# Sample attention over paged caches: a page on 64 partitions instead of 32

## The reference

```python
def mla_attend(q_lat, q_pe, q_pos, ckv, kpe, k_pos):
    s = (jnp.einsum("bqhc,bkc->bhqk", q_lat, ckv, preferred_element_type=jnp.float32)
         + jnp.einsum("bqhr,bkr->bhqk", q_pe, kpe, preferred_element_type=jnp.float32)) * MLA_SCALE
    s = jnp.where(k_pos[None, None, None, :] <= q_pos[None, None, :, None], s, -jnp.inf)
    p = jax.nn.softmax(s, axis=-1).astype(ckv.dtype)
    return jnp.einsum("bhqk,bkc->bqhc", p, ckv)
...
        ckv_past = cache_ckv[l, page_table].reshape(DB, past, KV_LORA)
        kpe_past = cache_kpe[l, page_table].reshape(DB, past, QK_ROPE)
```

## Time and profile before

| | us |
|---|---|
| time, median of 3 runs | 2335.02 (2325.26 to 2335.15) |
| profiled execution, its own time | 2333.65 |
| its span, first to last instruction | 2331.9 |
| PE busy | 2203.8 (95% of the span) |
| weight loads | 2010.6 (86%) |
| DVE, ACT, POOL busy | 1181.7, 831.7, 282.1 |

### The profile page before, as it was taken

One profiled execution on the slowest core, in us unless ns is written; L12 is line 12 of the kernel. 1 busy time (PEld: TensorE's weight loads), 2 busy tenths in 40 slices (PEclk: granted clock), 3 DMA queues, 4 the chain that ended last, 5 costly groups with the idle time before them and its releaser, 6 DMA issues.

```text
span 2331.9 us, 52276 instructions
## 1 busy us (share of the span) xinstructions
PE 2203.8 (95%) x22086; PEld 2010.6 (86%) x22086; DVE 1181.7 (51%) x1942; ACT 831.7 (36%) x1530; POOL 282.1 (12%) x275
## 2 busy tenths in 40 slices
PE   8989999999999999999999899999999989999997
PEld 7966667799998999999988666677999989999997
DVE  4732223533458763566667322244333687626665
ACT  4322223423235431234443222244232454313334
POOL 0012220000016000000340122200000340000002
PEclk9979999999999999999999799999999999999999
DMA  6167882022253222224432687800222522322252
GB/s 239 62 195 284 289 284 99 13 81 81 81 163 97 91 89 91 67 84 150 140 122 74 230 292 290 291 32 21 88 81 84 175 82 91 102 72 75 86 175 79
DMA packets 69362, 304.46 MB, mean 131 GB/s; under 512 B 8465, under 2 KB 13457, under 8 KB 56785
## 3 DMA queue, kind: packets, MB, share of 16 engines
q1 hardware_dynamic: 45360, 164.79, 22.0%
q0 software_dynamic: 18432, 125.84, 15.1%
q10 hardware_dynamic: 5408, 11.47, 1.5%
HBM read 294.02 MB, written 4.90 MB: 128 GB/s over the span
## 4 chain that ended last, share of the span: by engine, by line
PE 84%; DVE 7%; DMA 3%; ACT 2%; issue 2%; ACTq 0%; DVEq 0%; SPq 0%
PE PS L950 59%; PE PS L1206 7%; PE PS L1221 5%; DVE m_WL L1424 2%; PE PS L1190 2%; PE PS L1357 1%; DMA m_QSR<-m_QSF 1%; DMA m_WS<-in_w_units 1%; PE PS L1160 1%; PE PS L1184 1%; PE PS L1335 1%; PE PS L1346 1%; DVE m_X L1458 1%; DVE m_XL L1469 1%; ACT m_WH L511 1%
## 5 line engine op out<-in xcount | busy, mean ns | idle before, releaser
L950 PE MATMUL PS<-m_XH,m_WH 128*128 128x288 f32 x2560 | 733.5, 299 | 35.2 <-DVE m_WL L1424 19.4
L950 PE MATMUL PS<-m_XL,m_WH 128*128 128x288 f32 x2560 | 726.3, 296 | 0.0
L950 PE MATMUL PS<-m_XH,m_WL 128*128 128x288 f32 x2560 | 581.9, 297 | 0.0
L950 PEld LDWEIGHTS PS<-m_XH,m_WH 128*128 128x128 f32 x2560 | 485.1, 189 | 41.8 <-DVE m_WL L1424 22.8
L950 PEld LDWEIGHTS PS<-m_XL,m_WH 128*128 128x128 f32 x2560 | 485.8, 190 | 0.8
L1424 DVE TENSOR_TENSOR m_WL<-m_WS,m_WH 128x1024 fp32r<-128x1024 f32 (+2 forms) x284 | 369.0, 1301 | 230.3 <-ACT m_WH L511 220.4
L950 PEld LDWEIGHTS PS<-m_XH,m_WL 128*128 128x128 f32 x2560 | 424.6, 189 | 0.0
L511 ACT ACTIVATE m_WH<-m_WS 128x1024 fp32r<-128x1024 f32 (+2 forms) x284 | 315.1, 1112 | 299.2 <-PE PS L950 282.0
L950 PE MATMUL PS<-m_HH,m_WH 128*128 128x288 f32 x704 | 205.7, 299 | 7.7 <-DVE m_WL L1424 7.2
L950 PE MATMUL PS<-m_HL,m_WH 128*128 128x288 f32 x704 | 203.4, 296 | 0.0
L1206 PE MATMUL PS<-m_RAWF,m_QSR 32*64 32x128 f32 x4608 | 159.6, 285 | 27.9 <-issue 25.9
(11 more groups left out here) (287 smaller groups left out, 3315.2 us busy)
## 6 DMA issues: line engine op xcount, KB each, us to landing
m_WS<-in_w_units SPq DMA_DIRECT2D x232, 512.0 KB
m_WS<-in_w_units SPq DMA_DIRECT2D x48, 704.0 KB
m_WS<-in_w_units SPq DMA_DIRECT2D x4, 576.0 KB
out_y<-m_X SPq DMA_DIRECT2D x8, 288.0 KB, 2.2
m_QSR<-m_QSF ACTq DMA_DIRECT2D x4, 384.0 KB
m_RAWF<-in_cache_wide,m_IDXS POOLq DMA_INDIRECT x96
m_BRI<-in_branch_in ACTq DMA_DIRECT2D x2, 760.0 KB, 6.4
m_CST<-in_consts SPq DMA_DIRECT2D x1, 1425.5 KB, 12.6
```

Of the source, the lines that this page charges most:

```text
L950: mm = pe.matmul(out(half), w(part, k), x(k)[:, half_of(half)], start=(k == 0 and part == 0 and x is xh), stop=(k == last and part == 1))
```

## The change

A page now lies on 64 partitions. A gathered row holds the latent of two positions (512 numbers), 64 rotary numbers and, in the wide cache, 512 numbers by feature: a gather of 128 rows brings 2 pages, so a unit has **four gathers** of half the size, 576 or 1088 numbers a row, and `g_landed` counts four.

The by-feature keys stand in 4 groups of 64 features; the partitions 64h to 64h+63 hold page `h` of a gather. Scores of a group are 8 products of 128 columns on **four tiles of 64x64**, with `QSF` where the block matches and with one rotated copy `QSR` where it doesn't (two DMAs instead of six). The rotary part is on tiles of 32x64 still, 16 products of 64 columns a unit, in two parts `j` (the even and the odd positions); the second waits on a semaphore for the first's end (`even_mm`), now in units by feature too. A unit by feature has 32 + 16 products instead of 72. A unit by row has 16 rotary products instead of 8; its transposes, latent products and values are as many as before.

All scores now take two banks of 256 columns, in turn (`score_bank`): 0 and 1 for a unit by row, 2 and 3, then 0 and 1, then 4 and 5. So in every unit by feature two groups and half the rotary part stand ahead of the wait for `s_exp`, and in a unit by row half the key transposes do. DVE and ACT read two banks of 256 columns in every unit. On the host the caches are laid out anew, and the index list has 64 partitions to a page.

The core of the diff:

```diff
-GP = 4
+GP = 2
 NG = PAGES // GP
-NU2 = DB * NG // 2
+NQ = 4
+NU2 = DB * NG // NQ
 NF = 3
-ROW = 4 * KL + P
+HP = P // 2
+ROW = 2 * KL + HP
 KEYS_AT = ROW
-FROW = ROW + 8 * P
+FROW = ROW + 4 * P
...
-        RAWT = at("RAWT", [P, 2, ROW], F32, r_z + 6 * TB)
-        RAWF = [at(f"RAWF{n}", [P, 2, FROW], F32, o) for n, o in enumerate((r_xs, r_xs + 2 * FROW * 4, r_w))]
-        assert 4 * FROW * 4 <= 2 * DT * TB
-        QSR = [at(f"QSR{c}", [P, KT, 512], F32, r_w + 2 * FROW * 4 + (c - 1) * 4096) for c in range(1, 4)]
-        assert 2 * FROW * 4 + 3 * 4096 <= 6 * UW * 4
+        RAWT = at("RAWT", [P, NQ, ROW], F32, r_z + 6 * TB)
+        RAWF = [at(f"RAWF{n}", [P, NQ, FROW], F32, o) for n, o in enumerate((r_xs, r_xs + NQ * FROW * 4, r_w))]
+        assert 2 * NQ * FROW * 4 <= 2 * DT * TB
+        QSR = at("QSR", [P, KT, 512], F32, r_w + NQ * FROW * 4)
+        assert NQ * FROW * 4 + 4096 <= 6 * UW * 4
...
+        def score_bank(u):
+
+            return (0, 2, 0, 4)[u % 4]
+
+        def score_banks(u):
+
+            return PS[:, score_bank(u):score_bank(u) + 2, 0:256]
...
-                    for half in range(2):
-                        g = b * NG + half * 4 + j
+                    for q in range(NQ):
+                        g = b * NG + NQ * j + q
                         pool.indirect_dma_start(
-                            raw_of(u)[:, half, :], None, source.rearrange("l n c -> (l n) c"),
+                            raw_of(u)[:, q, :], None, source.rearrange("l n c -> (l n) c"),
                             bass.IndirectOffsetOnAxis(ap=IDXS[:, l, g:g + 1], axis=0))\
                             .then_inc(S[f"g_landed{u % 4}"], 16)
...
-                for c in range(1, 4):
-                    for to, at0, n in ((0, 32 * c, P - 32 * c), (P - 32 * c, 0, 32 * c)):
-                        act.dma_start(QSR[c - 1][to:to + n, :, :], QSF[at0:at0 + n, :, :]).then_inc(S["qs_turned"], 16)
+                for e in range(2):
+                    act.dma_start(QSR[64 * e:64 * e + 64, :, :], QSF[64 - 64 * e:128 - 64 * e, :, :])\
+                        .then_inc(S["qs_turned"], 16)
...
+                def rope_scores(u, j, start=False, stop=False):
+
+                    if j == 1:
+                        pe.wait_ge(S["even_mm"], l * NU2 + u + 1)
+                    rows_of = slice(u // 4 * 64, (u // 4 + 1) * 64)
+                    for half in range(2):
+                        for c in range(2):
+                            for h in range(2):
+                                rows = slice(64 * h + 32 * j, 64 * h + 32 * j + 32)
+                                at0 = half * P + j * HP
+                                mm = pe.matmul(PS[64 * c:64 * c + 64, score_bank(u) + h, at0:at0 + HP], QSP[rows, rows_of],
+                                               raw_of(u)[rows, 2 * half + c, 2 * KL:ROW],
+                                               start=(start and half == 0), stop=(stop and half == 1))
...
                 def scores_by_feature(u, groups):
 
-                    q = slice(u // 4 * 64, (u // 4 + 1) * 64)
+                    rows_of = slice(u // 4 * 64, (u // 4 + 1) * 64)
                     for g in groups:
-                        for s in range(4):
-                            rows = slice(32 * s, 32 * s + 32)
-                            if g < 8:
-                                ct, c = g // 4, (g - s) % 4
-                                weights = QSF[rows, ct, q] if c == 0 else QSR[c - 1][rows, ct, q]
-                                at0 = KEYS_AT + g * P
-                            else:
-                                weights, at0 = QSP[rows, q], 4 * KL
-                            for half in range(2):
-                                mm = pe.matmul(PS[64 * half:64 * half + 64, 2 + s, 0:P], weights,
-                                               raw_of(u)[rows, half, at0:at0 + P], start=(g == 0), stop=(g == 8))
-                    return mm
+                        for half in range(2):
+                            for c in range(2):
+                                for h in range(2):
+                                    rows = slice(64 * h, 64 * h + 64)
+                                    weights = (QSF if g % 2 == h else QSR)[rows, g // 2, rows_of]
+                                    at0 = KEYS_AT + g * P
+                                    pe.matmul(PS[64 * c:64 * c + 64, score_bank(u) + h, half * P:(half + 1) * P], weights,
+                                              raw_of(u)[rows, 2 * half + c, at0:at0 + P],
+                                              start=(g == 0 and half == 0), stop=False)
...
-                        rope_scores(u, (0, 2))
+                        rope_scores(u, 0, start=True)
+                        turn_keys(u, 0)
                         pe.wait_ge(S["s_exp"], l * NU2 + u)
-                        turn_keys(u, 0)
                         turn_probs(u - 1)
                         turn_keys(u, 1)
-                        rope_scores(u, (1, 3))
+                        rope_scores(u, 1)
                         scores(u)
-                    elif u % 4 == 1:
+                    else:
                         if u == 1:
-                            pe.wait_ge(S["qs_turned"], (l + 1) * 96)
-                        scores_by_feature(u, range(0, 5))
+                            pe.wait_ge(S["qs_turned"], (l + 1) * 32)
+                        scores_by_feature(u, (0,))
+                        rope_scores(u, 0)
+                        scores_by_feature(u, (1,))
                         pe.wait_ge(S["s_exp"], l * NU2 + u)
                         if u == 1:
                             pe.wait_ge(S["in_set"], l + 1)
                         turn_probs(u - 1)
-                        scores_by_feature(u, range(5, 9)).then_inc(S["s_mm"], 1)
-                    else:
-                        pe.wait_ge(S["s_exp"], l * NU2 + u)
-                        turn_probs(u - 1)
-                        scores_by_feature(u, range(0, 9)).then_inc(S["s_mm"], 1)
+                        scores_by_feature(u, (2, 3))
+                        rope_scores(u, 1, stop=True).then_inc(S["s_mm"], 1)
```

81 lines of the change are left out of this document (36 added, 45 removed).

## The result

The kernel after takes 2278.62 us (median of four, 2267.57 to 2280.5) where the kernel before takes 2331.79: a ratio of 0.9766, with a 95% interval of 0.974 to 0.9792. It is faster by 2.3%, where 2386 us was forecast. That is within 6 us of the lower end of rival A. The profiled execution has a span of 2275.9 us, 56.0 less than before's.

The account below looks back on a forecast made before the run. TensorE (PE) was taken as the bound, held back beside POOL's gathers. Per layer +25.8 feature units, +1.8 row units, +1.1 last units, -3.0 start gave +25.7; two layers +51 on 2335.0 made 2386 us, range 2295 to 2440.

Parts of the forecast that it names:

- rival A: Units by feature: slow stretch doesn't grow with the gathers, 2297 us, or disappears, 2273; chance 0.19.
- Supply: Units by feature: 100 records must precede the values, slowed until 6.05 us; 8.1 us a unit instead of 6.87.
- slow stretch: Sample attention: while POOL writes gathers, PE gets 7.4 records a us instead of over 60, after some 45 in reserve.
- rival B: Attention stage: PE's clock drops in the longer thin stretch, units lose 1.6 us, 2420 to 2453 us; chance 0.16.
- Gathers: POOL, each unit: four gathers of about 948 ns replace two, taking 4.7 us instead of 2.2.
- Own work: Units by feature, PE's work with nothing beside it: 5.4 us against 4.85 before, tile shape changes included.
- Unit by row: Eight more rotary products add 0.25 us to 6.8; bounds 0 and 0.8 us.
- Start of the stage: Wait on rotated query copies goes, VectorE's copies come next: about 3 us a layer saved, 0 to 4.
- Landing: Gather queue: four units of 7.9 MB in 31.3 us want 250 GB/s of 357, so no price.
- sign that half the packet size costs bandwidth: PE waiting for a gather's landing would show the forecast wrong; no size given.
- The lower end of the case: Units by feature at 7.4 us, with 100 records out by 5.35 us: +22 us, 2357 in all.
- Work ahead of the exponentials: Units by feature: new score banks let PE work ahead of this wait; worth little, 0.12 us stand there.

Follow-up runs that it names:

- after_again: Kernel after, unchanged, measured again: 2479.49 us, ratio 1.056 to the kernel before.
- before_again: Kernel before, unchanged, profiled again in one execution: 2317.37 us.
- session 3: Kernel after, unchanged (2479.49 us), and with its first rotary part moved behind the turned probabilities (2485.32 us), beside the kernel before at 2346.2 us.
- probs_first: Kernel after with the wait on the exponentials and the turned probabilities ahead of all scores in units by feature: 2492.93 us, ratio 1.0637.
- after_more: Kernel after, unchanged, measured a third time: 2287.66 us, ratio 0.9803 to the kernel before.
- pair_2: Kernel before with its latent score groups paired into products of 256 columns (wrong scores), rerun in another session: 2254.13 us, ratio 0.969.
- split_2: Kernel after with each score product cut into two of 64 columns, rerun in another session: 2332.82 us, ratio 1.0013.
- pair256: Kernel before with its latent score groups paired into products of 256 columns (wrong scores), first run: 2301.74 us, before 2356.78.
- four_half: Kernel before with each gather issued as two gathers of half rows, products unchanged: 2538.12 us, before 2356.78.
- held: Kernel before with each unit's gathers held until two thirds of the running unit's scores are out: 2350.94 us, ratio 1.0083.
- before_still: Kernel before without gathers for units by feature from unit 4 of a layer on (wrong result): 2375.73 us, before 2356.78.
- held_3: Kernel before with gathers held until two thirds of the running unit's scores are out, third run: 2379.24 us, ratio 1.0194.

## Why the prediction was wrong

**What failed** is the step named *Supply*. It took a slow stretch at 7.4 records a us with a reserve of 45 as a property of the two kernels, from one profiled execution, and let it grow with POOL's time to 6.05 us into the unit. The first profile of before ran in the way with the trickle. The measured result of after ran in the way without it, where four gathers hold nothing back and a unit takes 5.47 us (5.69 on average) instead of the 8.1 of the forecast. The weight of rival A (0.19) was set by which rows spoke for the slow stretch, and all rows came from one execution. The Trainium skill (Runtime: NRT & Kernel Launch, Instruction fetch mechanics), which states that the fetching of instructions is hidden, was set aside there because the 82.8 us of the earlier trace rows spoke against it; in the profile of after, 17.2 us at the score line agree with it, in after_again 118.9 do not. The 3.03 us in before_again, which end 1.40 us after a 16 KB packet of instructions, speak for a third case, in which the fetch of a block isn't hidden.

**Where the mechanism applies, it was undersized.** In session 3 the stop comes where forecast (a few dozen records after the first gather), but the unit takes 9.45 us and not 8.1 or 8.4. From the third gather on the pauses grow to 0.99 to 1.11 us, so about 3.4 records a us pass (5 in 0.46 and 0.99 us) and not 7.4, and rival B comes on top: the clock was 0.85 over the stage, and in some units the value products took 3.61 us, at 1.2 GHz, instead of 1.88. The unit by row, put at +0.25, took 8.20. So 2479 lies above even rival B's 2420 to 2453, which had the forecast's unit and the clock together.

**Point by point** otherwise, from the profile of after:

- *Gathers*: 256, of 947 and 957 ns in the median; forecast 948. Right.
- *Own work*: 5.4 us forecast, 5.47 measured; the last two units 5.4 forecast, 5.47 where they don't wait. Right, with the price of a change of tile shape in it. The sum took before's last two units at 4.85 each; the last one took 6.21 and 6.24 there, with the stops at 367 and 1521 us in it.
- *Unit by row*: +0.25 forecast, 6.77 measured. The rotary products cost nothing; the lower bound, 0, holds.
- *Start of the stage*: -3 us a layer forecast; -3.5 and -3.9 measured. The wait on the rotated copies is gone, and turning the first probabilities waits for VectorE, as named.
- *Landing*: not in the sum. The text had 22 us of queue for four units against 31 us that they would take. In the way that came, four units take 23.2 us of PE's time (3 x 5.47 + 6.77), and the waits for landings cost the 42 units 0.22 us each, 9 us in all. The prediction would have read such waits as a sign that half the packet size costs bandwidth; it costs little, 125.85 MB in 15.7% of 16 engines' span being 352 GB/s while busy, where before had 357. The queue simply has next to nothing to spare at 23.2 us for four units.
- *Rival A's 2273*: its sum over both layers was -62, and the stages gave -62.0, but by terms that cancel: 8 us less gained in the units by feature, 5 more in those by row, and 3 more at the start and in the last two units. The 5 us between 2273 and the 2277.88 of the profiled execution come from the 6 us given back outside of the stages.
- *The lower end of the case*: 7.4 us a unit doesn't follow from "100 are out by 5.35"; with values of 1.88 that is 7.2.
- *Work ahead of the exponentials*: no gain was forecast. probs_first differs from after_again by 13 us, but in two sessions and both with the trickle, so its price in the other way is open.

**The gain itself** is thus, in the way without the trickle, the end of the long stops and not a faster tile: before's own work is 4.88 us a unit where after's is 5.47, yet with its stops before takes 6.43 on average (before_again) against 5.72 (after_more). The 20 long stops of before_again hold 40 us; both stages together are 35 us shorter in after_more. Of the change, 116 records a unit instead of 164 is what counts: pair_2, with 100 and before's gathers, lost the long stops as well, and split_2, with 180 and after's gathers, got them back. In the way with the trickle the change costs 5.6%.

## What to carry to other kernels

A slow stretch that the profile puts down to nothing may belong to the session as much as to the kernel: profile the kernel before twice, on two occasions, before an argument rests on such rows, and give a rival by which it is missing the weight of an open question. Many small products (164 records a unit) are exposed in both ways, to stops behind packets of instructions and, in one way, to POOL's gathers; fewer, larger products on the same tiles helped in both (pair256), and more gathers beside them hurt in the one with the trickle (four_half). A change whose gain depends on the way, as this one does (0.977 and 0.980 against 1.056), should be measured in both before it is kept.

## What the runs showed of the hardware

- The same program with the same inputs has two ways of running in which units of one stage take 5.47 or 9.45 us; all profiled kernels of a session share the way.
- In the way with the trickle ACT and DVE start late as well: ACT's copies of the turned probabilities by 139 us in all in after_again, by 16 in after.
- In the trickle, pauses of 0.27 to 0.30 us with 5 or 6 records between them turn to pauses of 1.0 us where three or four gathers follow one another.
- A long stop ends 1.25 to 1.6 us after a 16 KB packet of instructions has passed. The longest, some 4 us, stand beside gathers (before_again, held); where no gather ran, they lasted 1.0 to 1.6 us (before_still).
- In before_still the clock was 0.60 and 0.50 in the 100 us behind the stage, where before had 1.00: the stage's gain of 27 and 23 us was lost there and more. A denser PE in the stage isn't shown to be the cause: held_3, with PE busy for 163 of the 200 us from 150 to 350, had 0.50 and 0.51 from 400 to 500 us in its profiled execution, and pair_2, with 186, had 1.00 and 0.90 from 350 to 450.
